# A decoder layer with 64 routed experts: the gathered rows come in four pieces of 32 partitions' width and are turned by VectorE

## The chip, the cores and the metric

The kernel runs on one core of a Trainium2 chip. The metric is the device time of one execution in microseconds (us). The engines are TensorE (PE; its weight loads are listed as PEld), VectorE (DVE), ScalarE (ACT), GpSimd (POOL) and SyncE (SP), which here only issues transfers. Transfers issued by SP run in the hardware queue q1, those issued by POOL in the software queue q0; both are served by the same 16 DMA engines.

## The reference

One layer of a hybrid decoder over 2048 tokens of 1024 features. The change concerns its mixture of experts; the attention, the recurrence and the projections before it are computed earlier in the kernel and are left as they are.

```python
def _moe(h, w_router, e_bias, w_gate, w_up, w_down, ws_gate, ws_up, ws_down):
    scores = jax.nn.sigmoid(hf.astype(f32) @ w_router.astype(f32))
    ...                       # each token picks 8 of 64 experts; wts are the weights of its 8 pairs
    def body(acc, blk):       # 128 rows of one expert at a time
        toks, bw, e = blk
        xb = hp[toks]
        yb = (jax.nn.silu(xb @ w_gate[e]) * (xb @ w_up[e])) @ w_down[e]
        return acc.at[toks].add(yb.astype(f32) * bw[:, None]), None
    ...
    shared = (jax.nn.silu(hf @ ws_gate) * (hf @ ws_up)) @ ws_down
    return (acc[:n_tok] + shared.astype(f32)).astype(h.dtype).reshape(bsz, seq, dm)
```

`w_gate` and `w_up` are 1024 x 256 for each expert and `w_down` is 256 x 1024, all float32. A block is 128 (token, expert) pairs of one expert; an expert whose count is no multiple of 128 has a last block with rows that stand for nothing.

## The kernel before

The part before the experts writes the table `htab` to DRAM: for each token its 1024 features and behind them its 64 routing weights, one row of 1088 numbers (`ROW_W`). `place_and_share` then computes for every block which tokens its 128 rows are (`idx`, one column for each block), the table of the order of the blocks, and the shared expert for the first eight tiles of tokens; it also gathers the first two blocks' rows. `experts` does all blocks, in a loop whose turn holds two steps (`TURN` = 2), one block finished in each step. The order on each engine is written out by hand, and the engines meet at semaphores. All products are made in float32 split into a high and a low part: high x high, high x low, low x high.

Step n of the loop works on several blocks at once:

- **TensorE** multiplies the low half of x of block n+1 with the gate and up weights (`gate_up_low`, L2514, 8 matmuls), the down projection of block n (L2559, 12 matmuls), the high half of x of block n+2 (`gate_up_high`, L2503, 16 matmuls), turns the hidden tile H of block n+1 (`turn_H`, L2521, two 128x128 transposes), and turns the gathered rows `xg` of block n+3 into two PSUM tiles `psX` (`turn_x`, L2487, eight 128x128 transposes).
- **ScalarE** copies the turned H out (`HT_hi`, L2389), the two halves of the turned x (`xT_hi`, L2340), makes the SiLU (L2376), for the first block of an expert splits off the high part of the next expert's weights (`gu_split` and `d_hi`, L2344), and copies one half of the result (`y`, L2395).
- **VectorE** makes the low parts: of H (`HT_lo`, L2466), of x (`xT_lo`, L2406, two halves out of PSUM), copies the pair weight of the next block out of `xg` (`pairw`, L2434), makes the gated product H (L2443), the low parts of the next expert's weights (L2409, three instructions per expert), and the other half of `y` (L2476).
- **GpSimd** copies a column of `idx` into `gi` (L2298), gathers the 128 rows of block n+4 with one indirect DMA (L2301), copies the column for the scatter (`si`, L2319), and adds `y` of block n into `acc` in DRAM with another (L2326). A row of `acc` may be met again by the next block, so each scatter waits for the landing of the one before it (`added`).
- **SyncE** loads the three weight matrices of the expert after next (L2284) when the low parts of the ones before them are made (`gulo_s`, `dlo_s`).

There are two buffers of `xg`, `xT_hi`, `xT_lo`, H, `psG`, `y` and of each weight. The gather of block n+4 waits until TensorE has turned block n+2:

```python
for n, s, k in steps(i):
    pool.wait_ge(turned[1], s.n + 3)
    pool.wait_ge(pairw_s, s.n + 3)
    gather(s.n + AHEAD, k, s.n + AHEAD + 1)
    ...
    pool.wait_ge(added[1 - k], (s.turn + k) * 16)
    nc.gpsimd.indirect_dma_start(out=acc, ..., compute_op=ALU.add).then_inc(added[k], 16)
```

## Time and profile before

| what | value |
|---|---|
| median of three runs | 2490.03 us (2484.62 to 2492.65) |
| the profiled execution | 2485.66 us, its span 2483.8 us |
| PE, DVE, ACT, POOL busy | 96%, 63%, 47%, 31% of the span |
| granted TensorE clock | 0.985 of full speed |
| DMA over the span | 524.34 MB, 211 GB/s |

The span is the time from the first to the last instruction in the profile of one execution. Busy shares are of the whole span; the loop of the experts takes from about 870 to about 2383 us in it.

### The profile page before, as it was taken

The numbers are of one execution on the slowest core, as the hardware profiler recorded it, in microseconds if no ns is written. First come the engines' busy times: TensorE is split into PE (matmuls) and PEld (weight loads), VectorE is DVE, ScalarE is ACT, GpSimd is POOL, SyncE is SP. The second block draws the span as 40 slices with busy tenths as digits, with TensorE's granted clock in tenths as the row PEclk, the third lists the DMA queues.
The fourth block names the chain that finished last, engine by engine and source line by source line (L and its number), as shares of the span: only waits on it lengthen the run. The fifth ranks groups of instructions, "written<-read, shape, count | busy, mean of one in ns | idle before, by whom it ended". The sixth has DMA issues, their size and how long they took to land. (4 is left out here: it accounts for less than half of the span.)

```text
span 2483.8 us, 49979 instructions
## 1 busy us (share of the span) xinstructions
PE 2382.5 (96%) x11840; PEld 1954.7 (79%) x11842; DVE 1575.5 (63%) x2285; ACT 1161.9 (47%) x1621; POOL 767.3 (31%) x829
## 2 busy tenths in 40 slices
PE   8899999989997799999999999999999999999986
PEld 6677777678886688888888888888888888888875
DVE  6686867768878756555665555656665556655447
ACT  4525253542225645445554445545554445544334
POOL 0010100011110134334543433534443334444327
PEclk9999999989998899999999999999999999999998
DMA  7242323364445579778988878888888789987863
GB/s 254 77 144 98 111 94 111 117 218 164 171 164 206 196 230 284 223 219 270 273 259 233 254 218 263 268 266 262 257 253 243 224 223 274 283 247 222 216 221 136
DMA packets 253808, 524.34 MB, mean 211 GB/s; under 512 B 18065, under 2 KB 165169, under 8 KB 249649
## 3 DMA queue, kind: packets, MB, share of 16 engines
q1 hardware_dynamic: 204464, 336.64, 39.7%
q0 software_dynamic: 48672, 186.86, 29.4%
q8 instruction: 36, 0.59, 0.1%
q14 instruction: 28, 0.22, 0.0%
q10 hardware_dynamic: 608, 0.02, 0.0%
HBM read 386.61 MB, written 136.87 MB: 211 GB/s over the span
## 5 line engine op out<-in xcount | busy, mean ns | idle before, releaser
L2503 PE MATMUL psG<-gu_split,xT_hi 128*128 x2624 | 624.3, 390 | 2.9 <-ACT xT_hi L2340 1.5
L2503 PEld LDWEIGHTS psG<-gu_split,xT_hi 128*128 128x128 f32 x2624 | 493.8, 188 | 106.2 <-issue 3.6
L2326 POOL DMA_INDIRECT acc<-y,si x162 | 290.1, 1791 | 728.6 <-DMA acc<-y,si 413.3
L2409 DVE TENSOR_TENSOR gu_split<-raw_gu,gu_split (+1 forms) x127 | 290.6, 2288 | 175.3 <-ACT gu_split L2344 171.7
L2514 PE MATMUL psG<-gu_split,xT_lo 128*128 x1304 | 339.3, 402 | 5.9 <-issue 5.8
L2514 PEld LDWEIGHTS psG<-gu_split,xT_lo 128*128 128x128 f32 x1304 | 233.1, 188 | 50.1 <-issue 8.7
L2344 ACT ACTIVATE gu_split<-raw_gu x126 | 234.3, 1907 | 33.5 <-issue 33.5
L2301 POOL DMA_INDIRECT xg<-htab,gi x164 | 205.0, 1250 | 130.4 <-POOL gi L2298 109.7
L2409 DVE TENSOR_TENSOR d_lo<-raw_d,d_hi (+1 forms) x64 | 146.7, 2292 | 149.5 <-ACT d_hi L2344 149.5
L2389 ACT ACTIVATE HT_hi<-psH 128x256 fp32r<-128x256 f32 x162 | 62.4, 385 | 351.6 <-PE psH L2521 351.6
L2406 DVE TENSOR_TENSOR xT_lo<-psX,xT_hi 128x512 fp32r<-128x512 f32 x328 | 209.7, 680 | 8.5 <-ACT xT_hi L2340 8.5
L2476 DVE COPY y<-psY 128x512 f32<-128x512 f32 x162 | 111.4, 688 | 154.0 <-PE psY L2559 154.0
L2559 PE MATMUL psY<-d_hi,HT_hi 128*128 x648 | 199.9, 390 | 0.0
L2559 PE MATMUL psY<-d_lo,HT_hi 128*128 x648 | 199.7, 389 | 0.0
L2559 PE MATMUL psY<-d_hi,HT_lo 128*128 x648 | 199.6, 389 | 0.0
L2340 ACT ACTIVATE xT_hi<-psX 128x512 fp32r<-128x512 f32 x328 | 178.5, 596 | 17.6 <-PE psX L2487 9.2
L2487 PE MATMUL psX<-ident,xg 128*128 128x128 f32 x1320 | 171.7, 273 | 4.2 <-PEq L1639 4.2
L2376 ACT ACTIVATE sg<-psG 128x256 f32<-128x256 f32 x163 | 62.6, 384 | 204.3 <-PE psG L2514 204.3
L2344 ACT ACTIVATE d_hi<-raw_d (+1 forms) x64 | 122.7, 1917 | 74.6 <-PE psY L2559 74.5
L2487 PEld LDWEIGHTS psX<-ident,xg 128*128 128x128 f32 x1320 | 149.3, 141 | 4.7 <-issue 4.6
L2466 DVE TENSOR_TENSOR HT_lo<-psH,HT_hi 128x256 fp32r<-128x256 f32 x162 | 67.8, 418 | 131.0 <-ACT HT_hi L2389 130.5
L2395 ACT ACTIVATE y<-psY 128x512 f32<-128x512 f32 x162 | 95.6, 590 | 102.5 <-PE psY L2559 98.4
(388 smaller groups left out, 3723.7 us busy)
## 6 DMA issues: line engine op xcount, KB each, us to landing
raw_gu<-in_w_gate_dram SPq DMA_DIRECT2D x64, 1024.0 KB, 6.0
raw_gu<-in_w_up_dram SPq DMA_DIRECT2D x64, 1024.0 KB
raw_d<-in_w_down_dram SPq DMA_DIRECT2D x64, 1024.0 KB, 6.9
wring<-split_d SPq DMA_DIRECT2D x24, 1024.0 KB, 4.8
split_d<-wring POOLq DMA_DIRECT2D x8, 1024.0 KB, 4.2
raw_d<-mixed SPq DMA_DIRECT2D x16, 512.0 KB, 3.9
xt<-in_x_dram SPq DMA_DIRECT2D x16, 512.0 KB, 4.3
htab<-h SPq DMA_DIRECT2D x16, 512.0 KB, 2.6
```

Of the source, the lines that this page charges most:

```text
L2301: nc.gpsimd.indirect_dma_start(out=xg[slot][:], out_offset=None, in_=htab, in_offset=bass.IndirectOffsetOnAxis(ap=gi[slot][:, 0:1], axis=0 ...
L2326: nc.gpsimd.indirect_dma_start(out=acc, out_offset=bass.IndirectOffsetOnAxis(ap=si[k][:, 0:1], axis=0), in_=y[k][:], in_offset=None, compu ...
L2340: nc.scalar.activation(xT_hi[slot][:, h * HALF:(h + 1) * HALF, :], psX[h][:], ACT.Copy).then_inc(xhi_s[h], 1)
L2344: nc.scalar.activation(dst, src, ACT.Copy).then_inc(done, 1)
L2395: nc.scalar.activation(y[k][:, 0:512], psY[:, 0, :], ACT.Copy).then_inc(y_s[0], 1)
L2406: nc.vector.tensor_tensor(xT_lo[slot][:, at, :], psX[h][:], xT_hi[slot][:, at, :], ALU.subtract).then_inc(xlo_s[h], 1)
L2409: nc.vector.tensor_tensor(dst, src, hi, ALU.subtract).then_inc(dlo_s if n == 2 else gulo_s, 1)
L2476: nc.vector.tensor_copy(y[k][:, 512:], psY[:, 1, :]).then_inc(y_s[1], 1)
L2487: m = nc.tensor.transpose(psX[half][:, c, :], xg[slot][:, (half * HALF + c) * P:(half * HALF + c + 1) * P], ident[:])
L2503: nc.tensor.matmul(psG[slot][:], xT_hi[slot][:, c, :], right[:, bass.ds(w, 1), c, :].rearrange("p a n -> p (a n)"), start=(n == 0 and c == ...
L2514: m = nc.tensor.matmul(psG[slot][:], xT_lo[slot][:, c, :], gu_hi[:, bass.ds(w, 1), c, :].rearrange("p a n -> p (a n)"), start=False, stop= ...
L2559: m = nc.tensor.matmul(psY[:, h, :], left[:, c, :], right[:, bass.ds(w, 1), c, h * 512:(h + 1) * 512].rearrange("p a n -> p (a n)"), start ...
```

## The change

The row of `htab` is laid out as four pieces of 272 numbers, each with 256 features and 16 routing weights. A block's rows are gathered by four indirect DMAs, each with 128 indices of its own (`gi` is now 128x4, out of `pidx`, which VectorE computes once from `idx` with 16 instructions on 32 partitions each). The indices are laid out so that 32 rows x 32 features stand in one square of 32x32; VectorE turns all squares of a block with two instructions (one for the features, one for the 64 routing weights with 64 zeros beside them) into `xF` in SBUF. A partition then holds features 8p to 8p+7, so the gate and up weights are loaded in the matching order of rows. TensorE only turns the tile of routing weights into `psW`, where VectorE picks the pair weight. ScalarE and VectorE make the high and low part of x from `xF`, each in one instruction. The copies of the indices move from GpSimd to ScalarE. VectorE's turn of block n+3 stands behind the product of step n.

```diff
+def gather_pieces(nc, htab, to, at, done):
+    for g in range(QUADS):
+        nc.gpsimd.indirect_dma_start(out=to[:, g, 0:PIECE], out_offset=None, in_=htab.rearrange("r a w -> (r a) w"),
+                                     in_offset=bass.IndirectOffsetOnAxis(ap=at[:, g:g + 1], axis=0)).then_inc(done, 16)
...
+                for a in range(QUADS):
+                    for g in range(QUADS):
+                        last = nc.vector.tensor_scalar(pidx[a * QP:(a + 1) * QP, :, g], idx[g * QP:(g + 1) * QP, :], float(QUADS), float(a),
+                                                       ALU.mult, ALU.add)
...
-                        sp.dma_start(dst, w[0, bass.ds(e, 1)].rearrange("a (k p) n -> p (a k) n", p=P)).then_inc(sm, 16)
+                        rows = "a (k p) n -> p (a k) n" if sm is down_in else "a (p k) n -> p (a k) n"
+                        sp.dma_start(dst, w[0, bass.ds(e, 1)].rearrange(rows, p=P)).then_inc(sm, 16)
...
-                    pool.wait_ge(turned[1], s.n + 3)
-                    pool.wait_ge(pairw_s, s.n + 3)
+                    pool.wait_ge(next_gi_s, s.n + 1)
                     carry_wait(pool, passed)
-                    gather(s.n + AHEAD, k, s.n + AHEAD + 1)
-                    nc.gpsimd.tensor_copy(si[k][:], idx[:, bass.ds(s.n, 1)]).then_inc(si_s, 1)
+                    gather_pieces(nc, htab, xg[k], gi[k], x_in[k])
                     s.wait(pool, si_s)
...
+            def gather_index(b, slot):
+                act.wait_ge(turned_s, b - 1)
+                carry_wait(act, passed)
+                nc.scalar.activation(gi[slot][:], pidx[:, bass.ds(b, 1), :].rearrange("p a g -> p (a g)"), ACT.Copy).then_inc(next_gi_s, 1)
...
-                    evac_x(s.n + 3, k)
+                    high_x(s.n + 3, k)
+                    gather_index(s.n + AHEAD, k)
                     silu(s.n + 2, 1 - k, s.n + 1)
...
-                    act.wait_ge(added[k], s.turn * 16)
+                    scatter_index(s, k)
...
+            def turn_x(slot, gathered, ahead):
+                dve.wait_ge(x_in[slot], gathered * 16 * QUADS)
+                if ahead is not None:
+                    dve.wait_ge(wturn_s, ahead)
+                    dve.wait_ge(xhi_s, ahead)
+                carry_wait(dve, passed)
+                nc.vector.transpose(xF[slot][:, 0:KC, :].rearrange("p c (g j) -> p c g j", g=QUADS),
+                                    xg[slot][:, :, 0:D // QUADS].rearrange("p g (i c) -> p c g i", c=KC))
+                nc.vector.transpose(xF[slot][:, KC, :].rearrange("p (g j) -> p g j", g=QUADS),
+                                    xg[slot][:, :, D // QUADS:WIDE]).then_inc(turned_s, 1)
+            def low_x(nth, slot):
+                dve.wait_ge(xhi_s, nth)
+                nc.vector.tensor_tensor(xT_lo[slot][:], xF[slot][:, 0:KC, :], xT_hi[slot][:], ALU.subtract).then_inc(xlo_s, 1)
...
-                    for h in range(2):
-                        evac_x(h, s.n + 3, k)
                     s.wait(dve, H_s)
-                    pair_weight(nexts[n + 1], k, s.turn + 2)
+                    pair_weight(nexts[n], s.n + 2, 1 - k)
+                    low_x(s.n + 3, k)
                     product(s.n + 2, 1 - k)
+                    turn_x(1 - k, s.turn + k + 2, s.n + 2)
...
-                    pe.wait_ge(x_in[1 - k], (s.turn + k + 2) * 16 )
-                    carry_wait(pe, passed)
-                    for h in range(2):
-                        pe.wait_ge(xlo_s[h], s.n + 3)
-                        turn_x(1 - k, h)
+                    turn_weights(s.n + 3, k)
```

Ahead of the loop, VectorE now turns the first blocks (its first turn stands ahead of the first split of weights, and waits for the last stores of `acc`). The stores of h and of the routing weights into `htab`, and the loads of h from it, go by pieces.

How the instructions move. GpSimd, one step of the expert loop before (`gi` and `si` are the columns of indices of the gather and the scatter):

```order
L2298 COPY gi<-idx 128x1
L2299 REGISTER_ALU
L2301 DMA xg<-htab,gi 128x1088
L2319 ISA
L2319 COPY si<-idx 128x1
L1099 REGISTER_ALU
L2324 REGISTER_ALU
L2326 DMA acc<-y_0,si 2176x1024
```

The same engine and two steps of the loop with the change:

```order
L1636 DMA xg<-htab,gi 128x272 x4
L2341 REGISTER_ALU
L2343 DMA acc<-y_0,si 2176x1024
L2335 REGISTER_ALU
L1636 DMA xg<-htab,gi 128x272 x4
L2341 ISA
L2343 DMA acc<-y_1,si 2176x1024
```

One gather and two copies of a step have become four gathers, and nothing else stands between two scatters.

VectorE, the head of a step before (`xT_lo` is the low part of the turned x, `H` the gated product, `psX` the PSUM tiles in which TensorE turned x):

```order
L2466 TENSOR_TENSOR HT_lo<-psH,HT_hi 128x256
L2404 REGISTER_ALU
L2406 TENSOR_TENSOR xT_lo<-psX_0,xT_hi 128x512
L2406 TENSOR_TENSOR xT_lo<-psX_1,xT_hi 128x512
L2432 ISA
L2434 REGISTER_ALU
L2434 ISA
L2434 COPY pairw<-xg 128x1
L2438 REGISTER_ALU
L2443 SCALAR_TENSOR_TENSOR H_1<-psG_1,pairw,sg 128x256
```

The same place with the change:

```order
L2506 TENSOR_TENSOR HT_lo<-psH,HT_hi 128x256
L2469 REGISTER_ALU
L2471 REGISTER_ALU x2
L2471 ISA
L2471 COPY pairw<-psW 128x1
L2442 REGISTER_ALU
L2443 TENSOR_TENSOR xT_lo<-xF,xT_hi 128x1024
L2480 SCALAR_TENSOR_TENSOR H_1<-psG_1,pairw,sg 128x256
L2431 ISA
L2436 STREAM_TRANSPOSE xF<-xg 128x1024
L2438 STREAM_TRANSPOSE xF<-xg 128x128
```

The two subtractions out of PSUM have become one that reads two SBUF tiles, and two turns stand behind the product; what splits the weights and copies `y` comes behind them, as before.

## Rows read from the trace of the kernel before

**Rows 1.** The page's slices of the span: busy tenths of PE, then DMA (40 slices).

```profile
PE   8899999989997799999999999999999999999986
...
DMA  7242323364445579778988878888888789987863
```

**Rows 2.** Timeline of PE, one step of the loop (start us, length us, engine, line).

```profile
1504.03 0.38 PE L2521 MATMUL psH<-ident,H 128*128 128x128 f32 x2
1504.24 1.04 PE L2487 MATMUL psX<-ident,xg 128*128 128x128 f32 x8
1505.04 2.07 PE L2514 MATMUL psG<-gu_split,xT_lo 128*128 x8
...
1509.67 3.79 PE L2503 MATMUL psG<-gu_split,xT_hi 128*128 x16
1513.30 0.38 PE L2521 MATMUL psH<-ident,H 128*128 128x128 f32 x2
```

**Rows 3.** The costliest groups of the page (count | busy, mean ns | idle before).

```profile
L2326 POOL DMA_INDIRECT acc<-y,si x162 | 290.1, 1791 | 728.6 <-DMA acc<-y,si 413.3
L2301 POOL DMA_INDIRECT xg<-htab,gi x164 | 205.0, 1250 | 130.4 <-POOL gi L2298 109.7
L2409 DVE TENSOR_TENSOR d_lo<-raw_d,d_hi (+1 forms) x64 | 146.7, 2292 | 149.5 <-ACT d_hi L2344 149.5
L2406 DVE TENSOR_TENSOR xT_lo<-psX,xT_hi 128x512 fp32r<-128x512 f32 x328 | 209.7, 680 | 8.5 <-ACT xT_hi L2340 8.5
```

**Rows 4.** The scatters of the loop, all 162: length ns, and time from issue to landing.

```profile
L2326 POOL DMA_INDIRECT acc<-y,si x162: 1583/1607/2717, 878.4 to 2381.2; - x162
...
DMA to landing us min/median/max: 6.0/7.5/11.4
```

**Rows 5.** Timeline of POOL in an expert of three blocks.

```profile
1506.97 1.60 POOL L2326 DMA_INDIRECT acc<-y,si  x1 [4.41 <-DMA acc<-y,si]
...
1509.58 1.01 POOL L2301 DMA_INDIRECT xg<-htab,gi  x1 [0.80 <-POOL gi L2298]
```

**Rows 6.** Timeline of POOL where experts of two blocks follow each other.

```profile
1535.25 1.61 POOL L2326 DMA_INDIRECT acc<-y,si  x1 [3.48 <-DMA acc<-y,si]
...
1546.31 1.60 POOL L2326 DMA_INDIRECT acc<-y,si  x1 [7.25 <-DMA acc<-y,si]
...
1551.06 2.85 POOL L2301 DMA_INDIRECT xg<-htab,gi  x1 [0.80 <-DVE y L2476]
...
1631.12 1.61 POOL L2326 DMA_INDIRECT acc<-y,si  x1 [3.13 <-DMA acc<-y,si]
```

**Rows 7.** Timeline of DVE at the same two places.

```profile
1517.42 0.47 DVE L2443 SCALAR_TENSOR_TENSOR H<-psG,pairw,sg 128x256 f32<-128x256 f32 x1
...
1550.74 2.28 DVE L2409 TENSOR_TENSOR gu_split<-raw_gu,gu_split  x1
...
1554.54 0.47 DVE L2443 SCALAR_TENSOR_TENSOR H<-psG,pairw,sg 128x256 f32<-128x256 f32 x1
```

**Rows 8.** DMA queues in 1512 to 1514, then 1523 to 1524 us: packets, MB, share.

```profile
q0 software_dynamic: 160, 0.59, 92.8%
...
q0 software_dynamic: 46, 0.19, 94.0%
q1 hardware_dynamic: 46, 0.05, 17.2%
```

**Rows 9.** DVE and PE just before the loop of the experts.

```profile
840.26 0.22 DVE L1947 TENSOR_SCALAR idx<-zr,blockno 128x4 int32<-128x4 f32 x1
841.02 2.29 DVE L2030 TENSOR_TENSOR gu_split<-raw_gu,gu_split 128x2048 fp32r<-128x2048 f32 x1 [0.54 <-ACT gu_split L1862]
844.17 1.22 DVE L1901 SCALAR_TENSOR_TENSOR out<-h,psY 128x1024 f32<-128x1024 f32 x1 [0.85 <-PE psY L2103]
845.30 0.34 DVE L1986 CAST table<-psO 1x196 int32<-1x196 f32 x1
```

**Rows 10.** Windows: us, PE, PEld, DVE, ACT, POOL busy, PEclk, DMA share, GB/s.

```profile
560.00:700.00 140.00, 140.00 (x743) 119.50 (x742) 115.37 (x211) 39.08 (x48) 19.33 (x20) 1.00 0.48 172
...
1290.00:1500.00 210.00, 210.00 (x1044) 176.57 (x1043) 116.69 (x161) 100.63 (x139) 81.05 (x90) 1.00 0.82 232
...
1540.00:1640.00 100.00, 97.37 (x483) 81.13 (x482) 63.40 (x78) 53.73 (x69) 48.32 (x40) 1.00 0.91 274
```

More of the change, by code:

```diff
@@ L2128, in _, with load_expert, experts @@
                     down(n)
-def load_expert(eng, w_gate, w_up, w_down, expert, slot, wgu, wd, loaded):
+def load_expert(eng, w_gate, w_up, w_down, expert, slot, wgu, wd, loaded, by_run=False):
     for w, sm, dst in zip((w_gate, w_up, w_down), loaded, (wgu[:, slot, :, 0:FE], wgu[:, slot, :, FE:], wd[:, slot])):
-        eng.dma_start(dst, w[0, expert].rearrange("(k p) n -> p k n", p=P)).then_inc(sm, 16)
-def experts(nc, passed, w_gate, w_up, w_down, ident, htab, acc, table, n_turns, idx, xg, gi, gi_s, x_in, acc_out, gu, guhi_s, gulo_s, wgu, wd, loaded, y, si, added,
+        rows = "(p k) n -> p k n" if by_run and w is not w_down else "(k p) n -> p k n"
+        eng.dma_start(dst, w[0, expert].rearrange(rows, p=P)).then_inc(sm, 16)
+def experts(nc, passed, w_gate, w_up, w_down, ident, htab, acc, table, n_turns, idx, pidx, tails_s, xg, gi, gi_s, x_in, acc_out, gu, guhi_s, gulo_s, wgu, wd, loaded, y, si, added,
             prefetch_shared, prefetch_hT):
@@ L2160, in experts @@
         xT_lo = [sb(f"xT_lo{i}", [P, KC, P], FR) for i in range(2)]
+        xF = [sb(f"xF{i}", [P, KC + 1, P]) for i in range(2)]
         sg = sb("sg5", [P, FE])
@@ L2203, in __init__, with column @@
                 self.word = word
-            def expert(self):
-                return within(self.word & (EXPERTS - 1), 0, EXPERTS - 1)
+            def column(self):
+                share = EXPERTS // QUADS
+                return within((self.word & (EXPERTS - 1)) + (self.word & (EXPERTS - share)), 0, P - 1)
             def next(self):
@@ L2535, in _ @@
             turn_H(0)
-            pe.wait_ge(x_in[0], 32)
-            for h in range(2):
-                pe.wait_ge(xlo_s[h], 2)
-                turn_x(0, h)
+            turn_weights(2, 1)
             def body(i):
@@ L3122, in decoder_layer @@
         si = [sb(f"si{i}", [P, 1], I32) for i in range(2)]
-        experts(nc, passed, w_gate, w_up, w_down, ident, htab, acc, table, n_turns, idx, xg, gi, gi_s, x_in, acc_out, gu, guhi_s, gulo_s, raw_gu, raw_d,
+        experts(nc, passed, w_gate, w_up, w_down, ident, htab, acc, table, n_turns, idx, pidx, tails_s, xg, gi, gi_s, x_in, acc_out, gu, guhi_s, gulo_s, raw_gu, raw_d,
                 loaded, y, si, added,
```

144 lines of the change are left out of this document (74 added, 70 removed).

## The prediction

> **What bounds the kernel now.** I read the slices of the page first: TensorE is busy nine tenths or more in nearly every slice from 870 us on, and the DMA engines stand at seven to nine tenths beside it [rows 1]. The experts' loop is 162 of the 164 steps that matter, so next comes PE's timeline of one step [rows 2]. It has no gap: from one turn of H to the next it is 1513.30 - 1504.03 = 9.27 us. In it the eight transposes of x hold the engine from 1504.24 to 1505.04, 0.80 us, or 0.10 us each (each is listed as longer because they overlap). TensorE sets the step, and the granted clock there is full [rows 10].
>
> Then I ask what stands close behind. The scatters wait for each other: 413 us of POOL's idle time is spent waiting for the landing of the last one [rows 3]. A scatter takes 6.0 to 11.4 us from issue to landing, 7.5 in the middle [rows 4], and the next cannot start before that. One short, one middle and one long landing make 24.9 us for an expert of three blocks, against 27.8 us of TensorE. Where experts have two blocks, ten scatters lie between 1535.25 and 1631.12 us [rows 6]: 95.9/10 = 9.59 us each, slower than TensorE's step, with PE down to 97.4 of 100 us and the DMA at 0.91 [rows 10]. So the second bound is very near, and in half of the experts it already holds: 64 experts share 162 blocks, which with two or three blocks each makes 30 of two (60 blocks) and 34 of about three (102 blocks).
>
> **The change, step by step.**
>
> *TensorE* does one transpose in place of eight: 7 x 0.10 = 0.70 us less of each of 162 steps, **-113 us** if nothing else takes its place. The step would be 9.28 - 0.70 = 8.58 us.
>
> *VectorE* loses two subtractions of 0.68 us and gains one of 1024 columns. A subtraction of 2048 columns from SBUF takes 2.29 us [rows 3], so half is 1.15. The turn of the features has no row; 1024 columns at that rate are 1.15 us as the lower bound, and twice that, 2.3 us, as the upper one should its stride of eight numbers halve the rate. I take 1.2, nearest the lower, since every full-width instruction in rows 3 and 9 runs near one column per ns, plus 0.2 for the small turn. Net: +1.2 us a step. The engine is busy 117 of 210 us in the loop, 5.2 us a step [rows 10]; 6.4 of 8.58 us still fits. ScalarE has one instruction in place of two and two tiny copies; at 101 of 210 us it has room, so nothing.
>
> *GpSimd*: four gathers for one. A gather takes 1.01 us undisturbed [rows 5]. With a scatter of 1.6 us that is 5.6 us of POOL's step; before, it was 1.6 + 1.0 + about 1.2 for the two copies and the wait between, 3.8 us. It fits within 7.5 us of landing. But the gather becomes complete 3.0 us later.
>
> *The gather's deadline* moves too, and this is the heart of my sum. Before, a gather issued at 1509.58 [rows 5] was read by TensorE at the end of the next step, 1522.81 us, 13.2 us later. Now VectorE wants it behind the product of that next step, which ended at 1517.42 + 0.47 = 1517.89 [rows 7], 8.3 us later, and 7.6 in a shorter step. The last of four issues ends 4.0 us after the first starts. What remains to the landing has no row for gathers, so I bound it. The least is the transfer of the last quarter: the queue moved 0.59 MB in 2 us [rows 8], so 0.5 us for 0.14 MB. The most is the scatter's shortest, 6.0 - 1.6 = 4.4 us after its issue, from a slower kind of transfer. The old gather's packets were served in 1512 to 1514 us, behind the scatter's, up to 3.4 us after its issue ended; I take that. So the rows come 4.5 to 8.4, likely 7.4 us after the first issue, where 7.6 are left: just in time. In the two-block stretch the gather started at 1551.06 and the product of the next step ended at 1555.01 [rows 6, 7], only 4.0 us later: there it will be late by 2 to 4 us. VectorE then stands still with `y`, the splits and `HT_lo` queued behind it, and TensorE waits for `HT_lo` and `y`. It has a reserve of some 3 us in a step without splits and little in one with them.
>
> *The shared port.* The gather at 1551.06 took 2.85 us where others take 1.01, and ended 0.89 us after the split of 1550.74 to 1553.02 ended [rows 6, 7]; so a gather that starts beside a VectorE instruction with two SBUF inputs first waits for its end. The new `xT_lo` is such an instruction, where the old one read PSUM; and four gathers meet a split more often than one. I charge it below, inside the lateness. The Trainium skill says this in "SBUF - State Buffer", Who interferes with whom: two SBUF inputs on VectorE block a GpSimd instruction that reads SBUF, and one input does not; the trace agrees with the first half, and no row shows the second, by which the turns themselves would be free of it.
>
> *The transfers.* 46 packets of each queue were served in the same us, 0.19 MB against 0.05 [rows 8]: the queues alternate by packet, whatever its size. Pieces of 1088 bytes instead of 4352 lose that advantage against weight loads, so a gather beside loads slows. Bytes are the same. By "DMA: Bandwidth & Descriptors", Queues, rings and completion order, of the Trainium skill the engines also alternate by packet, but with a packet of several descriptors; rows 8 show single ones, and I go by them. The gate and up loads write the same runs of 256 numbers in SBUF as before: nothing either way, covered by two experts' lead. The stores into `htab` fall in a stretch with the DMA at 0.48 [rows 10]: nothing; uncovered, they would cost at most a few us.
>
> *The start.* Sixteen index instructions of 196 columns (a cast of as many took 0.34 us [rows 9]; I take 0.27) are 4.4 us, of which some 1.4 falls into VectorE's idle time between 840.3 and 844.2 us: +3. The first turn ahead of the first split: +1.4. Together **+5 us**.
>
> **The sum.** -113. In the 60 two-block steps the scatters bound at 9.6 already: give back all of 0.70, +42, and 0.3 more each for late gathers and the port, +18. In the 34 experts of three blocks 24.9 us of landings fit in 25.8, but with no reserve; I charge 0.9 us an expert, a late gather in one of the three steps, +31. The start +5. Sum -17: 2485.7 - 17 = 2469 us for the profiled execution, which stands 4.4 below the median shown; **2473 us** on the scale of the medians. A difference under 0.3%, 7.5 us, cannot be told from none.
>
> **Rivals.**
> 1. *The full gain*: the gathers land within 2 us of their issue, and the scatters' landings shorten with less waiting. For it: landings have a minimum of 6.0, TensorE's own cut is certain. Against it: the 9.59 us between scatters above. 2490 - 113 + 5 = 2382, and with part of the two-block steps given back up to 2430.
> 2. *A full swap* (no change): the scatter chain holds everywhere, at about 9.2 a step, since less time for the same transfers lengthens the landings. 2483 to 2497.
> 3. *Slower, by the late gather*: VectorE waits for `x_in` in most steps. Mechanism: each step's gather starts only behind the scatter before it, four issues stretched by the port to 6 us, landing at 9 to 10 us where 7.6 are there; the wait of 2 us passes to `HT_lo` and TensorE. It decides from about 9 us between first issue and landing. A step of 9.5 to 9.6 us: 162 x 0.27 = +44, and the start: 2539. A turn at the upper bound of 2.3 us, or one that holds the port too, leads here as well.
> 4. *The turn does not replace the transposes' time*: TensorE might idle where the transposes hid something. Rows 2 show matmuls back to back with no such wait; this is part of case 2.
>
> **How the numbers follow.** My forecast, a part of the gain left (2440 to 2482): 0.35. The full gain (2380 to 2440): 0.16. No change: 0.14. Slower: 0.35, most of it up to 2545. Faster by over 0.3%: 0.51; within: 0.14; slower: 0.35. The range 2395 to 2545 leaves out half of the full gain's case and the tail of the slower one. The likeliest case's own range is 2440 to 2482.
>
> **What would show it.** Right: PE's step 8.6 us in three-block experts and 9.3 to 9.9 in two-block ones; a PE idle group released by `HT_lo`; a VectorE idle group before the turn of `xF` released by the gather, 100 to 250 us in all; POOL's waits on the landing of `acc` fewer than 413 us; a turn of 1.2 us. Wrong: no idle time before `xF` (rival 1), or over 300 us of it with steps of 9.5 throughout (rival 3), or a turn above 2 us.

## The result and the profile after

The change is slower: 2635.7 us (median of 4 runs, 2614.5 to 2636.9) against 2487.3 us for the kernel before, a ratio of 1.057 with a 95% interval of 1.052 to 1.063. The profiled execution spans 2635.0 us. The forecast was 2473, with a range up to 2545.

The page of the changed kernel, its slices for PE and DMA and the groups that answer to [rows 1, 3]:

```profile
PE   8899999899987789998989899889888988898886
...
DMA  6232231654563788788878778888887778887763
...
L1636 POOL DMA_INDIRECT xg<-htab,gi x664 | 859.2, 1294 | 213.8 <-issue 195.8
...
L2436 DVE STREAM_TRANSPOSE xF<-xg 128x1024 f32<-128x1024 f32 x165 | 351.9, 2133 | 308.0 <-DMA xg<-htab,gi 299.2
L2343 POOL DMA_INDIRECT acc<-y,si x162 | 313.7, 1936 | 288.2 <-DMA acc<-y,si 215.5
...
L2592 PE MATMUL psY<-d_hi,HT_hi 128*128 x648 | 228.9, 437 | 128.6 <-DVE y L2516 121.1
```

TensorE no longer fills its slices, and nothing took its place at nine tenths: the DMA engines moved down too. So no engine is busy all the time; the step is set by what waits for what. The gathers hold GpSimd for 859 us, where 164 of them took 205 [rows 3]. The turn is at 2.13 us, not 1.2. VectorE stood still 299 us for gathered rows, and TensorE 121 us for `y`, which VectorE makes behind the turn. The scatters' waits for each other fell from 413 to 215 us.

A stretch of 200 us of the change, with the columns of [rows 10]:

```profile
1200.00:1400.00 200.00, 179.60 (x763) 141.94 (x762) 150.52 (x162) 93.43 (x143) 137.49 (x97) 0.95 0.84 241
```

Before, the same stretch had TensorE at 198.8 us and GpSimd at 87.5. The granted clock was 1.00 and is 0.95: a mean over the two levels, 2.4 and 1.2 GHz. It was 1.00 from 1517 to 1525 us, where TensorE worked without a gap, and 0.66 from 1531 to 1535 us, behind 3.13 us in which it had stood idle. So it is below full where TensorE had waited, and adds to the waits. What it adds is inside the differences below, and no run separates it.

The 162 scatters mark the steps. Before, they start from 878.4 to 2381.2 us, 9.33 us apart; in the change from 893.8 to 2533.1, **10.18 us** apart. The loop gives 136 us and the start the rest: the first turn of `H` comes at 883.3 us instead of 869.7. Where nothing waits, the expected step is there: TensorE's turns of `H` at 1516.95 and 1525.47 us are 8.52 us apart. It is rare.

GpSimd's timeline of the change, two steps (start us, length us, what the engine waited for):

```profile
1510.49 2.29 POOL L2343 DMA_INDIRECT acc<-y,si  x1 [1.47 <-issue]
1513.08 0.99 POOL L1636 DMA_INDIRECT xg<-htab,gi  x1 [0.30 <-issue]
1514.38 2.60 POOL L1636 DMA_INDIRECT xg<-htab,gi  x1 [0.30 <-issue]
1517.28 2.49 POOL L1636 DMA_INDIRECT xg<-htab,gi  x1 [0.30 <-issue]
1520.07 1.23 POOL L1636 DMA_INDIRECT xg<-htab,gi  x1 [0.31 <-issue]
1521.61 1.62 POOL L2343 DMA_INDIRECT acc<-y,si  x1 [0.30 <-issue]
...
1531.37 2.29 POOL L2343 DMA_INDIRECT acc<-y,si  x1 [3.07 <-DMA acc<-y,si]
```

VectorE's timeline beside it:

```profile
1508.85 0.66 DVE L2516 COPY y<-psY 128x512 f32<-128x512 f32 x1
...
1513.87 2.27 DVE L2446 TENSOR_TENSOR gu_split<-raw_gu,gu_split  x1
1516.04 0.70 DVE L2516 COPY y<-psY 128x512 f32<-128x512 f32 x1
1516.64 2.30 DVE L2446 TENSOR_TENSOR gu_split<-raw_gu,gu_split  x1
...
1527.16 2.03 DVE L2436 STREAM_TRANSPOSE xF<-xg 128x1024 f32<-128x1024 f32 x1 [6.29 <-DMA xg<-htab,gi]
1529.12 0.27 DVE L2438 STREAM_TRANSPOSE xF<-xg 128x128 f32<-128x128 f32 x1
1529.31 0.65 DVE L2516 COPY y<-psY 128x512 f32<-128x512 f32 x1
```

Three paths lead from one scatter to a later one, and a scatter starts when the last of them is through.

- **The issues.** A scatter is issued at 1510.49. Behind it go four gathers, each beginning 0.30 us after the last one's end, and two of them take 2.6 and 2.5 us since they began beside a split (an L2446 instruction of VectorE, which makes a low part of the weights). The last ends at 1521.30, and the next scatter follows 0.31 us later, at 1521.61. Over the whole loop the train takes 6.1 us on average from the first issue's start to the last one's end, and in 53 of 161 steps the next scatter starts within 0.45 us of it.
- **The landing.** The scatter at 1531.37 waits for the landing of the one at 1521.61.
- **The ring through VectorE.** The rows of those four gathers are there at 1527.16, 5.9 us after the last issue and 14.1 us after the first. VectorE turns them, then makes `y`, which is ready at 1529.96; the scatter two steps on needs it. Where nothing else held a scatter it started 1.0 us behind `y`, as the one at 1510.49 did (`y` was ready at 1509.51). Here that would have been 1530.95, 0.4 us ahead of the landing.

That is 20.9 us for two steps, where TensorE needs 17.0. By the times in the trace, 88 of the 161 scatters start some 0.8 us after the landing before them, 52 start 0.3 us after the last issue, and 21 start 1.0 us behind `y`. So the ring through the turn and `y` is real, but it comes last in one step of eight; GpSimd's issues and the landings come last in the others. They hang together: a late scatter makes the gathers behind it, their rows and `y` late as well.

### The profile page after: what moved, and what is told of

The parts are those of the page before. It is cut to its first block and busy times, and to the rows that moved or that the text cites. A ratio compares the mean times of both kernels' runs of the same rounds, so it can differ in the third digit from the quotient of the medians.

```text
span 2635.0 us, 48189 instructions
## 1 busy us (share of the span) xinstructions
PE 2365.5 (90%) x10684; PEld 1867.5 (71%) x10686; DVE 1928.4 (73%) x2466; ACT 1166.5 (44%) x1781; POOL 1311.4 (50%) x1005
## 3 DMA queue, kind: packets, MB, share of 16 engines
q0 software_dynamic: 56640, 186.90, 28.6%
## 5 line engine op out<-in xcount | busy, mean ns | idle before, releaser
L1636 POOL DMA_INDIRECT xg<-htab,gi x664 | 859.2, 1294 | 213.8 <-issue 195.8
L2436 DVE STREAM_TRANSPOSE xF<-xg 128x1024 f32<-128x1024 f32 x165 | 351.9, 2133 | 308.0 <-DMA xg<-htab,gi 299.2
L2343 POOL DMA_INDIRECT acc<-y,si x162 | 313.7, 1936 | 288.2 <-DMA acc<-y,si 215.5
L2592 PE MATMUL psY<-d_hi,HT_hi 128*128 x648 | 228.9, 437 | 128.6 <-DVE y L2516 121.1
L2446 DVE TENSOR_TENSOR gu_split<-raw_gu,gu_split (+1 forms) x127 | 289.0, 2275 | 4.1 <-issue 4.1
L2592 PEld LDWEIGHTS psY<-d_hi,HT_hi 128*128 128x128 f32 x648 | 129.7, 209 | 179.7 <-issue 155.0
L2592 PE MATMUL psY<-d_hi,HT_lo 128*128 x648 | 229.1, 438 | 22.3 <-DVE HT_lo L2506 22.0
L2356 ACT ACTIVATE xT_hi<-xF 128x1024 fp32r<-128x1024 f32 x164 | 172.7, 1053 | 131.5 <-DVE xF L2438 128.8
L2443 DVE TENSOR_TENSOR xT_lo<-xF,xT_hi 128x1024 fp32r<-128x1024 f32 x164 | 199.9, 1219 | 15.4 <-ACT xT_hi L2356 9.5
L2592 PEld LDWEIGHTS psY<-d_hi,HT_lo 128*128 128x128 f32 x648 | 128.0, 209 | 75.8 <-issue 53.8
L2446 DVE TENSOR_TENSOR d_lo<-raw_d,d_hi (+1 forms) x64 | 146.0, 2282 | 35.9 <-ACT d_hi L2370 32.2
L2592 PEld LDWEIGHTS psY<-d_lo,HT_hi 128*128 128x128 f32 x648 | 134.7, 208 | 30.8
L926 PE MATMUL psP<-xT_hi,wring 128*128 128x512 f32 x512 | 130.1, 403 | 11.2 <-ACT xT_hi L444 3.6
```

The source lines that it names most:

```text
L926: m = nc.tensor.matmul(u.tile[:], w_[:, w, k, :], xT[x_][:, k, :], start=(n == 0), stop=(n == len(passes) - 1))
L1636: nc.gpsimd.indirect_dma_start(out=to[:, g, 0:PIECE], out_offset=None, in_=htab.rearrange("r a w -> (r a) w"), in_offset=bass.IndirectOffs ...
L2343: nc.gpsimd.indirect_dma_start(out=acc, out_offset=bass.IndirectOffsetOnAxis(ap=si[k][:, 0:1], axis=0), in_=y[k][:], in_offset=None, compu ...
L2356: nc.scalar.activation(xT_hi[slot][:], xF[slot][:, 0:KC, :], ACT.Copy).then_inc(xhi_s, 1)
L2436: nc.vector.transpose(xF[slot][:, 0:KC, :].rearrange("p c (g j) -> p c g j", g=QUADS), xg[slot][:, :, 0:D // QUADS].rearrange("p g (i c) - ...
L2443: nc.vector.tensor_tensor(xT_lo[slot][:], xF[slot][:, 0:KC, :], xT_hi[slot][:], ALU.subtract).then_inc(xlo_s, 1)
```

## The experiments

Fifteen kernels were run, each 4 to 12 times; times are medians. The ratios are to the kernel before, run beside them, and the brackets are 95% intervals.

In every kernel with one or two gathers (experiments 4 to 9 and 13) an index column that is used holds 32 rows, four times over, so the gathers read 32 or 64 different rows and not 128. In experiment 4 the queue moved as many bytes and packets as in the kernel before, and they took 28.9% of the span against 29.4%. What the repeated rows save is not separated.

### 1. Four pieces without the turn

The kernel before, with only its gather cut into four by columns; TensorE transposes as before, at the end of the step.

```
+    for g in range(QUADS):
+        nc.gpsimd.indirect_dma_start(out=to[:, g * PIECE:(g + 1) * PIECE], out_offset=None,
+                                     in_=htab.rearrange("r (a w) -> (r a) w", a=QUADS),
+                                     in_offset=bass.IndirectOffsetOnAxis(ap=at[:, g:g + 1], axis=0)).then_inc(done, 16)
```

> The kernel before with one part of the change alone: each block's rows come by four indirect DMAs of 272 numbers per row in place of one of 1088; TensorE still turns them at the end of the step, everything else stays. Theory G (the four gathers are slow to land, GpSimd holds four issues and their gaps, and the reader's place in the step only shows it): GpSimd takes 3.8 to 4 us more in a step, its waits on the landing of the scatter fall from 413 us, and in the runs of two-block experts TensorE begins to wait for x or y: 2500 to 2560 us. Theory P (only the reader's earlier place makes them late): the reader of 13 us later hides it all, 2485 to 2500 us. Theory V (the length of the turns on VectorE): no change, 2485 to 2495 us.

Measured: **2680.0 us**, a ratio of 1.075 (1.073 to 1.079). That is 120 us above the dearest theory. The cost of the gathers alone is larger than that of the whole change, and no reader in the middle of the step is needed for it. Three rows of GpSimd's timeline of this kernel:

```profile
1503.65 1.64 POOL L2338 DMA_INDIRECT acc<-y,si  x1 [0.90 <-POOL si L2331]
1505.96 0.19 POOL L2311 COPY gi<-pidx 128x4 int32 x1 [0.67 <-DVE pairw L2446]
1506.94 1.01 POOL L1634 DMA_INDIRECT xg<-htab,gi  x1 [0.79 <-POOL gi L2311]
```

Here GpSimd itself is the bound. On average over the loop the scatter takes 1.64 us, the copy of the indices and its waits 1.22 before the gathers, the train 6.47, and the copy and wait ahead of the next scatter 1.16: 10.49 us, which is the step. It waited for the landing of a scatter in only 14 steps. The two copies with their waits, 2.4 us a step, stand here on GpSimd and in the change on ScalarE, so the two kernels differ in more than the turn.

### 2. The turn's stride

The change, with the squares read from adjacent numbers instead of every eighth.

```
-  xg[slot][:, :, 0:D // QUADS].rearrange("p g (i c) -> p c g i", c=KC)
+  xg[slot][:, :, 0:D // QUADS].rearrange("p g (c i) -> p c g i", c=KC)
```

> The changed kernel, whose turn reads each square's 32 numbers side by side in place of eight apart; features then meet the wrong weights' rows, so the routed experts' output is not the reference's, while every instruction, transfer and wait is kept. Theory V (the turn at 2.13 us is long because of its stride): the turn falls to 1.1 to 1.3 us, VectorE has 0.9 us less in a step, and 60 to 150 us of the 148 lost come back: 2490 to 2575 us. Theory G: VectorE would only wait longer for the gather, 2610 to 2640 us, with the idle time before the turn up from 299 to over 400 us.

Measured: **2602.8 us**, 1.045 (1.044 to 1.047), between the ranges of the two theories: 33 us of the loss is the stride. Part of it passes through GpSimd: its scatters take 1.78 us to issue here and 1.94 in the change, 25 us over the loop. The turn of this kernel:

```profile
L2436 DVE STREAM_TRANSPOSE xF<-xg x164: 1227/1245/1248, 869.1 to 2502.1; 128x1024 f32<-128x1024 f32 x164
```

In the change the same line reads 1991/2159/2270 ns. With a step of 32 bytes between numbers it takes 1.7 times as long. The Trainium skill ("SBUF - State Buffer", the note on cachelines in its part on the DMA port swizzle) has lines of 16 bytes, and a penalty for each access that goes to a new one; the direction agrees, and the page gives no figure for it.

### 3. The turn at the end of VectorE's step

> The changed kernel with VectorE's turn moved from behind the product to the end of the step, behind the splits and the copy of y. Theory P: the rows have 3 to 8 us more to come, the 299 us of idle time before the turn falls under 60 us, and most of the loss goes, 2450 to 2530 us. Theory V: the amount of VectorE's work is the same, and in the steps with splits the turn now comes so late that ScalarE's high part and with it TensorE wait for it: 2600 to 2680 us. Theory G: partly better, 2560 to 2610 us.

```
                     product(s.n + 2, 1 - k)
-                    turn_x(1 - k, s.turn + k + 2, s.n + 2)
...
+                    turn_x(1 - k, s.turn + k + 2, s.n + 2)
```

Measured: **2727.3 us**, 1.095 (1.093 to 1.097). Every theory had less; the place behind the product was the better one. VectorE now waits little for rows, but ScalarE's `xT_hi` waited 483 us for the turn: it is late for TensorE's next step.

### 4. One gather

The change, with one indirect transfer of rows of 1088 numbers.

```
-    for g in range(QUADS):
-        nc.gpsimd.indirect_dma_start(out=to[:, g, 0:PIECE], out_offset=None, in_=htab.rearrange("r a w -> (r a) w"),
+    nc.gpsimd.indirect_dma_start(out=to[:].rearrange("p g w -> p (g w)")[:, 0:QUADS * PIECE], out_offset=None,
+                                 in_=htab.rearrange("r a w -> r (a w)"),
```

> The changed kernel with one indirect DMA of whole rows of 1088 numbers in place of four of pieces; the squares then hold the wrong rows, so the routed output is not the reference's, while the turns, their place and all else stay. Theory G: GpSimd takes 4 us less in a step, the rows land 4 us sooner, the idle time before the turn falls from 299 us to under 80, and 80 to 150 us come back: 2485 to 2555 us. Theory V: VectorE's 2.4 us of turns stay, and so does most of the loss: 2590 to 2630 us.

Measured: **2482.3 us**, 0.997 (0.996 to 0.998). Cutting the row into four gathers holds 153 us of the loss. But the rest of the change is worth 7 us only, not 113. GpSimd's waits in this kernel name what took the gain:

```profile
engine line waited for: us in total, times, longest us
POOL acc L2343 <- DMA acc<-y,si: 861.5, 144, 7.6
...
DVE xF L2436 <- DMA xg<-htab,gi: 145.0, 89, 3.2
```

In 144 of 161 steps the scatter waited for the landing of the last one. Its issue took 1.90 us on average, the landing came 6.44 us later, and the next scatter began 0.85 us behind that: 9.19 of the 9.24 us between scatters.

### 5. Issues or small pieces?

The one-gather kernel, with three more indirect transfers of 8 numbers a row into a spare tile.

```
+    for g in range(1, QUADS):
+        nc.gpsimd.indirect_dma_start(out=spare[:, g, :], out_offset=None,
+                                     in_=htab.rearrange("r a (b w) -> (r a b) w", w=8),
+                                     in_offset=bass.IndirectOffsetOnAxis(ap=at[:, g:g + 1], axis=0)).then_inc(done, 16)
```

> The changed kernel with one indirect transfer of whole rows of 1088 numbers (as in e4_one_gather), followed by three more indirect transfers that fetch 8 numbers a row into a spare tile. So GpSimd issues four indirect transfers a step as the change does, with 1.26 us from one to the next, but the rows still move as packets of the old size and the added data is 12 KB a step. (The squares hold wrong rows, as in e4.) VectorE's turn waits for all four, as in the change. Theory G, the number of issues costs, by GpSimd's time, its waits at the shared port and the later end of the last issue: near the changed kernel, 2600 to 2650 us. Rival S, the small pieces cost (packets of 1088 bytes that alternate one for one with the weight loads): near e4, 2480 to 2500 us. Half way between, 2540 to 2570, if both.

Measured: **2606.9 us**, 1.048 (1.043 to 1.053). So 125 of the 153 us come with the issues, though they carry almost nothing, and the other 29 with the rows in four pieces. The 29 are the difference of two medians whose single runs reach from 2602 to 2625 and from 2614 to 2637 us: they are small against their noise. The loop's figures are nearly the change's: 9.96 us a step, and 273 us of waiting before the turn.

### 6. Two gathers

```
+    for g in range(2):
+        nc.gpsimd.indirect_dma_start(out=flat[:, g * wide:(g + 1) * wide], out_offset=None,
+                                     in_=htab.rearrange("r (a b) w -> (r a) (b w)", a=2),
```

> The changed kernel with two indirect transfers of 544 numbers a row in place of four of 272 (the squares hold wrong rows). Packets of 2176 bytes. The traces of e4 (one) and of the change (four) give 2482 and 2636 us. In e4 the scatters bound the step at 9.24 us with 6.0 us between the end of the gather and the next scatter; a second issue adds 1.26 us to GpSimd and to the gather's end. Theory G with a threshold (the added issues are free until the gather's lateness passes to the scatter through VectorE): 2485 to 2520 us. A cost in proportion to the number of issues, 51 us for each: 2533 us. If the port stalls set the cost (about one issue in five stalls by 1.6 us): near 2510.

Measured: **2493.4 us**, 1.0015 (1.0001 to 1.0029), 11 us above one gather and not 51, as the theory with a threshold had it. The train of 2.6 us still ends 4.4 us ahead of the next scatter, and the landing of the last scatter ends later than it in 135 steps. Four gathers of 6.1 us leave 1.8.

### 7 and 8. What eats the gain when the gather is one

The one-gather kernel with the adjacent read of experiment 2, and with even and odd blocks added into two arrays:

```
-  pool.wait_ge(added[1 - k], (s.turn + k) * 16)
-  nc.gpsimd.indirect_dma_start(out=acc, out_offset=bass.IndirectOffsetOnAxis(ap=si[k][:, 0:1], axis=0),
+  nc.gpsimd.indirect_dma_start(out=(acc, acc_odd)[k], out_offset=bass.IndirectOffsetOnAxis(ap=si[k][:, 0:1], axis=0),
```

> The one-transfer kernel e4 with the turn reading its squares from adjacent numbers, so that it takes about 1.24 us in place of 2.16 (features meet wrong rows of the weights, and the squares hold wrong rows). In e4 the scatter waited for the landing of the one before it in 144 of 161 steps, 861 us in all. Theory C, the chain of scatters bounds e4: VectorE's 0.9 us a step buys nothing, 2470 to 2485 us. Rival V, the turn's double duration is still in the way: 30 us less as between the change and e2, or more, 2400 to 2455 us.

> The one-transfer kernel e4 with even blocks added into acc and odd blocks into a second array of the same size, so a scatter need not wait for the landing of the one before it, only for the one before that. (The odd blocks' part is left out of the output, and the squares hold wrong rows.) Bytes and transfers are the same. Theory C, the wait for each other's landing bounds e4: PE's step falls to 8.6 to 8.8 us, 2375 to 2410 us: the full gain appears. Rival B, the transfers' own bandwidth bounds (the DMA engines were busy 0.8 to 0.9 of the time): 2450 to 2482 us.

Measured: **2430.9 us** (0.977, 0.975 to 0.980) and **2415.9 us** (0.970, 0.968 to 0.972). The second is 6 us above the range of theory C: a scatter's wait for the landing before it is worth 66 us, and bandwidth is not the bound. The first lies in rival V's range, but the trace shows theory C's chain still in place. In this kernel 158 of the 161 scatters start some 0.8 us after the landing before them, as 143 did in experiment 4, and they are 8.93 us apart instead of 9.24. The chain itself became shorter. Its scatters take 1.67 us to issue where those of experiment 4 took 1.90, for fewer begin beside a VectorE instruction with two SBUF inputs (15 were longer than the usual 1.6 us by over 0.3, against 61): 0.225 x 162 = 36 of the 51 us lie there, and some 11 more in landings that come 0.07 us sooner. So VectorE's shorter turn acts by when GpSimd's issues meet VectorE's other work.

### 9. Late rows or an occupied GpSimd?

Experiment 5, with the turn waiting for the whole-row transfer alone.

```
-  in_offset=bass.IndirectOffsetOnAxis(ap=at[:, g:g + 1], axis=0)).then_inc(done, 16)
+  in_offset=bass.IndirectOffsetOnAxis(ap=at[:, g:g + 1], axis=0)).then_inc(free, 16)
```

> e5_thin, but the three thin transfers raise a semaphore of their own, so VectorE's turn waits for the whole-row transfer alone, which is the first of the four. (The squares hold wrong rows.) GpSimd's time is that of e5, the rows' time is that of e4. Theory L, lateness: what costs is that the last issue ends 4 us later and the rows with it, so that VectorE's turn and behind it y, the next scatter and the next gathers are late: nearly e4's time, 2485 to 2520 us. Rival O, occupation: GpSimd's 6 us of issues between two scatters delay the scatters by themselves: near e5, 2580 to 2610 us.

Measured: **2564.3 us**, 1.032 (1.029 to 1.034). The time lies between the two theories: of the 125 us, 43 go with the rows' lateness and 82 stay with GpSimd's time. The division is rough, for GpSimd's time was not the same: all gathers together hold it 952.8 us here and 840.7 in experiment 5, since 271 of them are longer than 1.2 us against 161, and ScalarE's copy of the indices also waits for the thin transfers, 10 us in all. In 89 of 161 steps the scatter now starts within 0.45 us of the last issue, and it waits for the landing of the last scatter in only 51.

### 10 and 11. The kernel before, with less in its scatters' way

Two arrays in the kernel before, and its two index copies made by ScalarE:

```
-  nc.gpsimd.tensor_copy(si[k][:], idx[:, bass.ds(s.n, 1)]).then_inc(si_s, 1)
+  nc.scalar.activation(si[k][:], idx[:, bass.ds(s.n, 1)], ACT.Copy).then_inc(si_s, 1)
```

> The kernel before with odd blocks added into a second array, so that a scatter waits for the landing of the one before the last alone. (The odd blocks' part is left out of the output.) In its trace the scatter waited for the one before it in 77 of 161 steps, 413 us, and TensorE's step without a wait is 9.28 us against 9.33 on average. The theory of the prediction, that in two-block experts the scatter chain of 9.6 us bounds: 20 us less, 2465 to 2475 us. Rival: PE bounds everywhere and the chain only fills its slack: 2485 to 2495 us.

> The kernel before with the two index copies of a step made by ScalarE, as the change has them, in place of GpSimd: nothing else. GpSimd loses 0.8 to 1.0 us before each gather and 0.2 us behind it. TensorE bounds the kernel before, so the theory expects no change: 2480 to 2495 us. Rival: the scatters wait for GpSimd in part of the steps, and a shorter GpSimd step gives 5 to 20 us: 2470 to 2482 us.

Measured: **2480.3 us** (0.9963, 0.9950 to 0.9975) and **2482.4 us** (0.9970, 0.9955 to 0.9985). The scatters' chain costs the kernel before about 9 us, half of what the prediction's own theory had said, though 413 us of waits are shown for it. The copies on ScalarE are a gain of 8.5 us, small, but with an interval that ends below 1: of the versions that compute the whole layer this is the fastest one found, ahead of both kernels.

### 12. An adjacent turn with the loads to match

```
+  for g in range(QUADS):
+      eng.dma_start(wgu[g * QP:(g + 1) * QP, slot, :, at],
+                    w[0, expert, g * QP * KC:(g + 1) * QP * KC].rearrange("(k i) n -> i k n", i=QP)).then_inc(sm, 16)
```

> The changed kernel with the turn reading adjacent numbers, and the gate and up weights laid to match: each load as four transfers of 32 partitions whose rows of 1 KB come from 32 neighbouring rows at a time. The output is the reference's. e2_contig, the same turn without the loads, took 2603 us. Theory: the loads have two experts' lead, so the four issues instead of one cost nothing: 2595 to 2615 us. Rival: SyncE's eight issues an expert in place of two, or the 32-partition transfers, delay loads or scatters: 2620 to 2660 us.

Measured: **2705.3 us**, 1.087 (1.085 to 1.090), 102 us above experiment 2, far outside the theory. The page's queue of the loads, in this kernel and then in experiment 2:

```profile
q1 hardware_dynamic: 226096, 336.67, 46.1%
```

```profile
q1 hardware_dynamic: 219952, 336.64, 39.2%
```

The same bytes held the DMA engines for a sixth more of a span that is itself longer: 46.1% of 2702.7 us is 1246 us, 39.2% of 2609.4 us is 1023. The engines are at 0.98 in 1200 to 1400 us, and VectorE waited 500 us for rows. The Trainium skill ("SBUF - State Buffer", Door 1: The DMA port swizzle) says that a transfer's speed hangs on how many of the 16 ports its partitions reach, and 32 neighbouring ones reach eight; the trace agrees in direction. The order in which the rows are read from memory changed as well, and which of the two costs more was not tried.

### 13 to 15. The gain, the ring, and its tightest link

> The three suspects out at once: one transfer of whole rows, the turn reading adjacent numbers, and odd blocks added into a second array (whose part is left out of the output; squares and weights meet wrong rows). Singly, from e4's 2482, the adjacent read gave 51 us and the second array 66. If the prediction's -113 of TensorE is all there once nothing else bounds, the time is 2490 - 113 + 10 for the later start = 2387, so the two together give 95 and not 117: 2380 to 2400 us. Rival: something else still bounds (VectorE, ScalarE or the loads), and the two do not add: 2405 to 2416 us, as e8.

Measured: **2385.6 us**, 0.957 (0.955 to 0.960). This is 108 us below the kernel before, and the forecast of 2387 was worked out from TensorE's cut and the late start alone. The scatters are 8.65 us apart, 0.07 over the step that was forecast, and all of them start behind `y`: with the issues, the stride and the landings out, little is left. The hit is partly luck. The second array alone gives the kernel before 9 us (experiment 10), and against that kernel this one gains 95 us, which with a start 10 to 14 us later makes 105 to 109 of the 113.

> The change itself, with odd blocks added into a second array (their part is left out of the output), so that no scatter waits for the landing of the last one. In the change's trace that wait came to 215 us in 75 steps. Theory G, GpSimd's issues and the late rows close the loop of the change, and the wait for landings only fills in: 20 us or less of gain, 2610 to 2640 us. Rival C, the scatter chain is a member of the loop (scatter, gathers behind it, turn, y, scatter): 60 us or more of gain, below 2575 us.

Measured: **2506.3 us**, 1.006 (1.004 to 1.009), 129 us below the change with all four gathers and the slow turn in place. Theory G fell, clearly. But the gain is not the wait alone. All gathers together hold GpSimd 665.9 us here, against 859.2 in the change, and the train of four takes 4.9 us instead of 6.1, since only 37 of the gathers, and not 162, are longer than 1.2 us; the scatters take 393.5 us instead of 313.7. So the scatters' new places also moved the gathers away from the splits. How the 129 us divide between the two is not shown.

The last one puts two pieces ahead of the scatter and two behind.

```
-  gather_pieces(nc, htab, xg[k], gi[k], x_in[k])
+  gather_pieces(nc, htab, xg[k], gi[k], x_in[k], range(2))
...
+  gather_pieces(nc, htab, xg[k], gi[k], x_in[k], range(2, QUADS))
```

> The change with two of the four gathers ahead of the step's scatter and two behind it; the output is the reference's. A scatter now waits for two issues at most instead of four, but the last two pieces follow the scatter in the queue. Theory Q, pieces behind a scatter land only after it (a scatter takes 8 us to land) and the rows' lateness is what VectorE feels: slower, 2660 to 2720 us. Rival O, what costs is the scatter's delay by the issues: faster than the change, 2590 to 2620 us.

Measured: **3429.1 us**, 1.376 (1.373 to 1.380). The direction is theory Q's, the size nobody's. GpSimd's timeline of it, and VectorE's:

```profile
1508.88 2.71 POOL L2343 DMA_INDIRECT acc<-y,si  x1 [8.88 <-DVE y L2517]
...
1513.20 0.95 POOL L1636 DMA_INDIRECT xg<-htab,gi  x1 [0.31 <-issue]
...
1524.35 2.72 POOL L2343 DMA_INDIRECT acc<-y,si  x1 [7.69 <-DVE y L2517]
```

```profile
1520.59 2.00 DVE L2437 STREAM_TRANSPOSE xF<-xg 128x1024 f32<-128x1024 f32 x1 [8.57 <-DMA xg<-htab,gi]
```

The last pieces now wait in GpSimd's order behind a scatter that waits for `y`, and `y` stands in VectorE's order behind a turn that waits for those pieces. What was a ring over two steps is one over a single step: scatter 2.7, two issues 2.6, landing 6.4 (1520.59 - 1514.15), the turns, `y` and what lies between 3.8, together 15.5 us a step. All 161 scatters of this kernel start behind `y`. In the change the same ring spans two steps, and only 21 do.

## Why the prediction was wrong

The pieces, by differences of medians:

| from | to | us | what it is |
|---|---|---|---|
| before | experiment 13 | -108 | TensorE's seven transposes, with the later start (and 9 us of the second array) |
| 13 | 8 | +30 | the turn's stride, with each scatter free of the landing before it |
| 8 | 4 | +66 | the scatters' wait for each other's landing |
| 4 | 9 | +82 | three more issues: GpSimd's time, roughly |
| 9 | 5 | +43 | the same: rows late for the turn |
| 5 | the change | +29 | rows in four pieces (near the noise) |

They make +142; the change is 142 to 148 us above the kernel before, whose medians lie between 2487 and 2493 us. They hold in this order only: taken from the change itself, the landings' wait is 129 us and the stride 33.

By the prediction's own steps:

- **TensorE, -113.** Right in the main: 8.58 us was forecast for a step, 8.52 stands in the trace of the change where nothing waits, and experiments 10 and 13 together show 105 to 109 of the 113 us.
- **VectorE, a turn of 1.2 us.** Wrong choice between two bounds given: 2.13 us, near the upper of 2.3. The rows that ran near one column per ns all read adjacent numbers. It alone is 33 us, and would have taken the forecast from 2473 to 2506.
- **GpSimd, "it fits within 7.5 us of landing": this is the step that failed.** Four issues at 1.01 were counted back to back. They stand 0.30 us apart, which no row of before could show, and begin beside the splits so often that the train is 6.1 us and not 4.0. A scatter, the train and the two gaps around it make 1.94 + 0.30 + 6.11 + 0.30 = 8.65 us, more than the 8.58 that a step was to last, before any wait for a landing. The prediction priced the issues by the gather's lateness and put GpSimd's own time at nothing; three more issues cost 125 us (experiments 4 and 5), of which experiment 9 gives some 82 to the time and 43 to the lateness.
- **The deadline, 7.4 us where 7.6 are left.** The mechanism was right and stood in rival 3; the size was not. From first issue to rows it is 7.3 us or less for the gathers of 1504 us, but 12.4 and 14.1 for those that VectorE waited for at 1506 and 1527 us. The landing was bounded by 4.4 us after the last issue; it was 5.3 and 5.9 there.
- **The shared port.** The rule read from one row held: of some 640 gathers in the change, 129 began beside a split and took 2.59 us on average, 1.6 more than the others; all but one lasted until at least 0.8 us after the split's end. The new `xT_lo` does the same on a smaller scale: 34 gathers began beside it and took 1.24 us. It was charged "inside the lateness", that is, at next to nothing, where it is some 210 us of GpSimd's time, against 40 in the kernel before. The turn itself does no harm there. 222 gathers began beside one and took 0.96 us as elsewhere, such as this one:

```profile
1508.08 0.95 POOL L1636 DMA_INDIRECT xg<-htab,gi  x1 [0.30 <-issue]
```

The turn beside it:

```profile
1506.57 2.17 DVE L2436 STREAM_TRANSPOSE xF<-xg 128x1024 f32<-128x1024 f32 x1 [5.67 <-DMA xg<-htab,gi]
```

This is the half of the rule in "SBUF - State Buffer" of the Trainium skill, Who interferes with whom, that no row of before showed: one SBUF input does not hold the port.

- **The transfers.** That pieces of 1088 bytes would be packets of 1088 bytes is not what the trace shows. The queue of the gathers moved the same 186.9 MB in 56640 packets, before in 48672: the 7968 more are 16 for each of the 498 added transfers, small ones. From 1517 to 1519 us only gathers were served, with 35 packets of about 4.3 KB and 24 tiny ones:

```profile
DMA packets 59, 0.15 MB, mean 76 GB/s; under 512 B 24, under 2 KB 24, under 8 KB 59
```

So the packets kept their size of before, one for four pieces, where the prediction took [rows 8] to mean one for each piece; there was no advantage to lose in the alternation. That a gather beside loads is slow may hold for another reason. The last issue of the late gather ended at 1521.30, and from 1522 to 1524 us the loads had the engines alone:

```profile
q1 hardware_dynamic: 749, 0.77, 109.1%
```

Why its rows were not served then is open, and so is where the 29 us come from.

- **Two-block experts, +42 and +18.** The scatters' chain was seen, but as a bound of half of the experts at 9.6 us. With TensorE's step shorter and one gather it is one in nearly all (144 of 161 steps of experiment 4), at 9.24 us. That the sum of 60 came near the 66 us of experiment 8 is luck. The chain is no fixed rate either: experiment 7 shortened it by 0.3 us a step through VectorE. In the kernel before it costs 9 us (experiment 10).
- **The start, +5.** It was +13.6. The sixteen index instructions take 0.35 us each and not 0.27, 5.6 us together, and TensorE stood still for 5.3 us behind them; then the eight gathers fill GpSimd from 850.45 to 860.57 us, and the first turn starts at 864.16.

Rival 1, the full gain at 2382, is near what experiment 13 shows once the obstacles are out (2385.6), and rival 4, that TensorE would idle in place of the transposes, falls with it. Rival 2, the full swap with the scatters 9.2 us apart, is the change with a single gather (2482.3, 9.24 us). Rival 3 was the outcome, at 0.35, with a price of 2539. It had the train of 6 us right and the step at 9.5 to 9.6 where it is 10.18, so it was too cheap by 97 us. It let the lateness pass only to `HT_lo` and TensorE; in the trace the scatters' own issues and landings hold most steps, and each late scatter makes the next gathers late. How the 97 us divide among these is not shown.

## What to carry to other kernels

Add up the step of every engine that issues transfers, gaps included, also when it was mostly idle before: here GpSimd was busy 31% of the span, and three more issues filled its step. Then follow each wait around: where A's output feeds B, B's feeds C, and C's stands ahead of A's next turn in some engine's order, add up the ring and divide by the steps of lookahead; the step is the longest of these paths. Don't take a wait that the profile shows for its worth: the waits for the scatters' landings were 413, 861 and 215 us in the kernel before, in experiment 4 and in the change, and taking them away gave 9, 66 and 129. Count indirect transfers by number, not by bytes: here one more cost 11 us and three more 125. And try the kernel before with the change's cheapest-looking part alone (experiment 1 here): it showed at once that the four gathers cost more than the whole change.

## What the hardware showed that was not expected

- An indirect transfer of 128 rows holds GpSimd 0.95 us and the next begins 0.30 us later, whether it carries 139 KB (the change) or 4 KB (experiment 5): 1.26 us each in a train, where no split is in the way.
- An indirect transfer whose issue began beside a VectorE instruction with two SBUF inputs lasted until 0.8 us after that instruction's end (gathers) or 1.5 us after it (scatters); beside a turn, with one SBUF input, it took 0.96 us.
- Gathers of 1088 bytes a row were recorded as packets of 4352 bytes, as were those of whole rows.
- A 32x32 turn of 128x1024 float32 numbers takes 1.24 us from adjacent numbers and 2.13 to 2.16 us with a step of eight.
- Loads cut into four of 32 partitions held the DMA engines 1246 us instead of 1023 for the same 337 MB.
- Two of four gathers moved behind the scatter cost 793 us, more than any other edit here.
